# Turning raw exponentials in forgetting and latent attention, and dividing by their sums after the value product

## What is computed

```
sb = (jnp.einsum('bhqd,bhkd->bhqk', sl(qb), kb).astype(jnp.float32) * scale
      + (c_q[..., None] - cum[:, :, None, :]))
pb = jax.nn.softmax(jnp.where(causal, sb, -jnp.inf), axis=-1)
ob = jnp.einsum('bhqk,bhkd->bhqd', pb.astype(vb.dtype), vb)
```

```
s = (jnp.einsum("bqhd,bkhd->bhqk", qn, k_nope)
     + jnp.einsum("bqhr,bkr->bhqk", qp, k_pe)).astype(jnp.float32) * MLA_SCALE
s = jnp.where(kpos[None, :] <= qpos[:, None], s, NEG)
p = jax.nn.softmax(s, axis=-1).astype(v.dtype)
return jnp.einsum("bhqk,bkhd->bqhd", p, v)
```

## Time and profile before

| | |
|---|---|
| median of 3 runs | 2430.66 us |
| span of the profiled execution | 2425.54 us |
| TensorE busy | 2388.7 us (98%) |
| VectorE, ScalarE, GpSimd busy | 51%, 39%, 41% |
| chain that ended last | TensorE 91%, VectorE 3%, ScalarE 2% |
| fox, first score to last value product | 194.67 to 362.81 us: 168.14 us |
| mla0, the same | 1708.04 to 1762.10 us: 54.06 us |
| mla1, the same | 1788.81 to 1843.37 us: 54.56 us |

### The profile page before, as it was taken

One profiled execution on the slowest core, in us unless ns is written; L12 is line 12 of the kernel. 1 busy time (PEld: TensorE's weight loads), 2 busy tenths in 40 slices (PEclk: granted clock), 3 DMA queues, 4 the chain that ended last, 5 costly groups with the idle time before them and its releaser, 6 DMA issues.

```text
span 2425.5 us, 29219 instructions
## 1 busy us (share of the span) xinstructions
PE 2388.7 (98%) x10762; PEld 1877.3 (77%) x10762; DVE 1237.2 (51%) x2086; ACT 952.3 (39%) x1438; POOL 1000.8 (41%) x744
## 2 busy tenths in 40 slices
PE   8999999999999999999999999999989999999999
PEld 6777668877888888857878888887556877888887
DVE  4453545334334436794456455556765334555454
ACT  3354345433322226524444222226766434222223
POOL 4323224333454445635425554544021233554443
PEclk9999999999999999999999999999999999999999
DMA  5212213421322233222223223232102421322331
GB/s 171 87 53 83 83 43 122 157 87 53 126 91 100 88 103 104 87 70 88 86 59 103 100 92 104 87 104 68 36 18 87 147 97 53 107 93 88 102 104 70
DMA packets 169703, 218.31 MB, mean 90 GB/s; under 512 B 6584, under 2 KB 143338, under 8 KB 169590
## 3 DMA queue, kind: packets, MB, share of 16 engines
q1 hardware_dynamic: 168278, 214.59, 27.2%
q10 hardware_dynamic: 1312, 2.21, 0.3%
HBM read 214.66 MB, written 2.12 MB: 89 GB/s over the span
## 4 chain that ended last, share of the span: by engine, by line
PE 91%; DVE 3%; ACT 2%; issue 1%; POOL 1%; DMA 1%; SPq 0%; DVEq 0%; ACTq 0%
PE ps_l L839 78%; PE ps_l L1096 3%; PE ps_l L988 2%; PE ps_s L1146 2%; PE ps_l L1222 1%; POOL w_lo L685 1%; PE ps_s L1205 1%; ACT w_hi L1444 1%; PE ps_s L1309 1%; PE ps_s L1324 1%; PE ps_s L1111 1%; DVE small L2752 0%; PE ps_s L839 0%; DVE arena L2235 0%; DVE a_lo L2287 0%
## 5 line engine op out<-in xcount | busy, mean ns | idle before, releaser
L685 POOL TENSOR_TENSOR w_lo<-w_raw,w_hi 128x512 fp32r<-128x512 f32 (+1 forms) x740 | 1000.6, 1384 | 1403.5 <-ACT w_hi L1444 1385.7
L839 PE MATMUL ps_l<-a_hi,w_hi 128*128 128x512 f32 x1936 | 763.6, 394 | 2.9 <-POOL w_lo L685 2.8
L839 PE MATMUL ps_l<-a_lo,w_hi 128*128 128x512 f32 x1952 | 758.4, 389 | 0.0
L839 PE MATMUL ps_l<-a_hi,w_lo 128*128 128x512 f32 x1936 | 754.1, 390 | 0.0
L1444 ACT ACTIVATE w_hi<-w_raw 128x2048 fp32r<-128x2048 f32 (+2 forms) x196 | 370.6, 1891 | 587.7 <-PE ps_l L839 579.5
L839 PEld LDWEIGHTS ps_l<-a_hi,w_hi 128*128 128x128 f32 x1936 | 363.0, 188 | 88.0 <-issue 10.8
L839 PEld LDWEIGHTS ps_l<-a_lo,w_hi 128*128 128x128 f32 x1952 | 366.0, 187 | 78.0 <-issue 3.1
L839 PEld LDWEIGHTS ps_l<-a_hi,w_lo 128*128 128x128 f32 x1936 | 362.7, 187 | 77.3
L839 PE MATMUL ps_l<-b_hi,w_hi 128*128 128x512 f32 (+1 forms) x892 | 329.4, 369 | 6.2 <-POOL w_lo L685 3.8
L839 PE MATMUL ps_l<-b_hi,w_lo 128*128 128x512 f32 (+1 forms) x892 | 326.7, 366 | 0.0
L839 PE MATMUL ps_l<-b_lo,w_hi 128*128 128x512 f32 (+1 forms) x892 | 326.7, 366 | 0.0
(11 more groups left out here) (294 smaller groups left out, 2509.1 us busy)
## 6 DMA issues: line engine op xcount, KB each, us to landing
w_raw<-in_ffn_w_up_dram SPq DMA_DIRECT2D x44, 1024.0 KB, 5.0
w_raw<-in_w_dram SPq DMA_DIRECT2D x32, 1024.0 KB, 5.2
w_raw<-in_ffn_w_down_dram SPq DMA_DIRECT2D x22, 1024.0 KB, 4.9
w_raw<-in_w_in_dram SPq DMA_DIRECT2D x20, 1024.0 KB, 5.3
w_raw<-in_xa_wkv_dram SPq DMA_DIRECT2D x16, 1024.0 KB, 5.5
w_raw<-in_w_kv_mem_dram SPq DMA_DIRECT2D x8, 1024.0 KB, 5.6
w_raw<-in_xa_wq_dram SPq DMA_DIRECT2D x8, 1024.0 KB, 5.1
w_raw<-in_xa_wo_dram SPq DMA_DIRECT2D x8, 1024.0 KB, 5.2
```

The lines of the kernel that those rows point to most:

```text
L685: e.tensor_tensor(w_lo[:, b % 2, o], w_raw[:, b % 2, o], w_hi[:, b % 2, o].bitcast(F32), ALU.subtract).then_inc(w_lo_made[by], 1)
L839: ins = pe.matmul(o, *((v, w) if swap else (w, v)), start=first and n == 0, stop=last and n == 2)
```

## The change

Both attentions turn the raw exponentials, not the divided ones, and the division by the sums comes after the value product. For that the value product is made the other way round: the turned block is the stationary operand and the values (64 columns) move, 10 products per head, so that the result has queries on its rows. VectorE multiplies it with the reciprocals of the sums while it takes it out of PSUM (P), TensorE turns the result back (a new event W, four tiles for two heads), and O and the low part (Q) work on two heads at once, 128 x 512.

In fox two heads become one event: 16 steps, not 32; S scores both heads of a pair one after the other on the upper and the lower 64 rows of the array; T turns both; the lag is 2 steps; the fills are dealt out anew over the 19 steps. The rows of sums come for two heads in one DMA, with a small one ahead for block 0.

In mla heads stay single; the lag is 2 steps instead of 3, V follows T of the last block by one event step and stands behind T of the next head's block 0; P two steps after T, W and O (for odd heads) two, Q three. The buffers for exponentials and for turned blocks are doubled, so exponentials no longer wait for the turning of the head before.

```diff
+def latent_events(heads, lag):
+    for step in range(n + lag + 4):
+        for kind in "PQ":
+            if (step, kind) in due:
+                ev.append((kind, due[step, kind], 0))
+        if step < n:
+            ev.append(("S", *divmod(step, TT)))
+        for kind in "WO":
+            if (step, kind) in due:
+                ev.append((kind, due[step, kind], 0))
+        if lag <= step < n + lag:
+            h, i = divmod(step - lag, TT)
+            ev.append(("T", h, i))
+            if i == TT - 1:
+                due[step + 1, "V"] = due[step + 2, "P"] = h
+                if h % 2:
+                    due[step + 2, "W"] = due[step + 2, "O"] = due[step + 3, "Q"] = h // 2
+        if (step, "V") in due:
+            ev.append(("V", due[step, "V"], 0))
...
-    attention("fox", FOX_HEADS, 3, "v", 1, extra="K", after=(2, 2, 3), fills=(
+    attention("fox", FOX_HEADS, 2, "v", 2, extra="K", after=(1, 2, 2, 3, 3), pairs=True, fills=(
...
+            def pair_values(g, p, _):
+                claim(pe, L, g)
+                wait_read(pe, L, plan.events["fox"][1]["T", p, TT - 1] + 1)
+                for i, e in itertools.product(range(TT), (0, 1)):
+                    o = P * i + 64 * e
+                    for k in range(i + 1):
+                        ins = pe.matmul(bank(L, g)[:, o:o + 64], pt_pair(i)[:, e, k, :],
+                                        vb[:, k, (2 * p + e) * 64:(2 * p + e + 1) * 64], start=k == 0, stop=k == i)
+                ins.then_inc(l_full, 1)
+            def pair_values_turned(g, p):
+                claim(pe, L, g)
+                wait_read(pe, L, plan.events["fox"][1]["V", p, 0])
+                for i in range(TT):
+                    ins = turn(bank(L, g)[:, i * P:(i + 1) * P], o_fox(p)[:, i, :])
+                ins.then_inc(l_full, 1)
...
+            def masked_scores(g, i, both):
+                n = P * (i + 1)
+                for e, (q, k) in enumerate(both):
+                    claim(pe, S, g + e)
+                    pe.matmul(bank(S, g + e)[:, 0:n], q, k[:, 0:n] if n < T else k, start=True, stop=False)
+                for e in (0, 1):
+                    pe.matmul(bank(S, g + e)[:, i * P:n], ident_bf[:, :], mask_bf[:, :], start=False, stop=True)\
+                        .then_inc(s_full, 1)
...
+                    if kind == "V":
+                        claim(pe, L, g)
+                        wait_read(pe, L, at["T", h, TT - 1])
+                        for q in range(TT):
+                            for k in range(q + 1):
+                                ins = pe.matmul(bank(L, g)[:, 64 * q:64 * q + 64], pt_lat(h, q, k),
+                                                vh[:, k, h * 64:(h + 1) * 64], start=k == 0, stop=k == q)
+                        ins.then_inc(l_full, 1)
...
+                    if kind == "P":
+                        wait_read(dve, S, at["S", h, TT - 1])
+                        rl4, l = lat_sum[:, 4 * TT:5 * TT], TT * (h % 4)
+                        step(dve.reciprocal(rl4, lat_sum[:, l:l + TT]))
+                        wait_group(dve, L, g)
+                        if h >= 4:
+                            wait_group(dve, L, at["W", h // 2 - 2, 0])
+                        sync()
+                        dve.tensor_tensor(o_lat(h // 2)[:, :, 64 * (h % 2):64 * (h % 2) + 64],
+                                          bank(L, g)[:, 0:4 * 64].rearrange("p (q d) -> p q d", d=64),
+                                          rl4.unsqueeze(2).broadcast_to((P, TT, 64)), ALU.mult).then_inc(l_free["v"], 1)
```

More of the change, by code:

```diff
@@ L122, in attention_events, with pair_events, turned_groups @@
     return ev
+def pair_events(pairs, lag, extra, after, fill):
+    ev = []
+    n = pairs * TT
+    due = {}
+    for step in range(n + lag + 8):
+        if step < n:
+            p, i = divmod(step, TT)
+            if "K" in extra and step == 0:
+                ev.append(("K", 0, 0))
+            ev.append(("S", p, i))
+            if "K" in extra and p and i == 0:
+                ev.append(("K", p, 0))
+            if "K" in extra and i == 1 and p + 1 < pairs:
+                ev.append(("K", p + 1, 1))
+        for kind in "POQ":
+            if (step, kind) in due:
+                ev.append((kind, due[step, kind], 0))
+        for item in fill.get(step, ()):
+            ev.append(("G", item, 0))
+        for kind in "WV":
+            if (step, kind) in due:
+                ev.append((kind, due[step, kind], 0))
+        if lag <= step < n + lag:
+            p, i = divmod(step - lag, TT)
+            ev.append(("T", p, i))
+            if i == TT - 1:
+                for kind, wait in zip("VPWOQ", after):
+                    due[step + wait, kind] = p
+    return ev
+def turned_groups(i):
+    return 1 if i < 2 else 2
+def latent_events(heads, lag):
+    ev = []
+    n = heads * TT
+    due = {}
+    for step in range(n + lag + 4):
+        for kind in "PQ":
+            if (step, kind) in due:
+                ev.append((kind, due[step, kind], 0))
+        if step < n:
+            ev.append(("S", *divmod(step, TT)))
+        for kind in "WO":
+            if (step, kind) in due:
+                ev.append((kind, due[step, kind], 0))
+        if lag <= step < n + lag:
+            h, i = divmod(step - lag, TT)
+            ev.append(("T", h, i))
+            if i == TT - 1:
+                due[step + 1, "V"] = due[step + 2, "P"] = h
[3 more added lines that the diff above has]
+            ev.append(("V", due[step, "V"], 0))
+    return ev
 class Plan:
@@ L195, in attention @@
     def attention(name, heads, lag, score_who, per_score, t_who="a", v_who="v", v_groups=1, extra="",
-                  after=(3, 3, 4, 3, 3), fills=(), halves=()):
+                  after=(3, 3, 4, 3, 3), fills=(), halves=(), pairs=False):
         fill = {}
@@ L201, in attention @@
                 fill.setdefault(step, []).append((tag, *divmod(n, parts), parts))
-        ev = attention_events(heads, lag, extra, after, fill, halves)
+        ev = pair_events(heads // 2, lag, extra, after, fill) if pairs else \
+            attention_events(heads, lag, extra, after, fill, halves)
         at = {}
@@ L214, in attention @@
                 at[kind, h, i] = len(L.who)
-                L.who += [t_who]
+                L.who += [t_who] * (turned_groups(i) if pairs else 1)
             elif kind == "V":
@@ L223, in attention @@
                     L.who += [next(who for t, *_, who, _, _ in fills if t == tag)]
-            elif kind in "OPN":
-                at[kind, h, i] = at["V", h, i]
+            elif kind in "OPNQ":
+                at[kind, h, i] = at["W" if pairs and kind in "OQ" else "V", h, i]
         p.events[name] = (ev, at)
@@ L328, in make_plan @@
         p.weights(f"uk{half}", "mla_w_ukv_2", 2, 1024, [(0, 1024 * half)], 8)
-        attention(f"mla{half}", 8, 3, "a", 1)
+        ev, at = latent_events(8, 2), {}
+        for kind, h, i in ev:
+            ring, who = {"S": (S, "a"), "T": (L, "a"), "V": (L, "v"), "W": (L, "v")}.get(kind, (None, ""))
+            if ring:
+                at[kind, h, i] = len(ring.who)
+                ring.who.append(who)
+            else:
+                at[kind, h, i] = at["V" if kind == "P" else "W", h, 0]
+        p.events[f"mla{half}"] = (ev, at)
     feat_around("mla_o", "mla_w_o_2", [0, 256, 512, 768], "memT2")
@@ L1062, in _, with attention @@
             ins.then_inc(s_full, 1)
-            def attention(name, score, values, before=None, turned=None, subln=None, fills={}):
+            def attention(name, score, values, turned=None, subln=None, values_turned=None, fills={}):
                 ev, at = plan.events[name]
@@ L2281, in half_values, with walk_pairs @@
[L2281 to L2288, removed]
+            def walk_pairs(scores, evict, low, filled):
+                ev, at = plan.events["fox"]
+                for kind, p, i in ev:
+                    g = at[kind, p, i]
+                    if kind == "S":
+                        scores(g, p, i)
+                    if kind == "G" and ring_who(g) == "v" and p[2] == p[3] - 1:
+                        filled(g, *p[0:2])
+                    if kind == "P":
+                        evict(g, p)
+                    if kind == "Q":
+                        low(g, p)
```

235 lines of the change are left out of this document (170 added, 65 removed).

## The result

The changed kernel takes 2493.07 us (median of four runs, 2489.25 to 2493.46) against 2430.55 us: +62.5 us, a ratio of 1.0252 (95% interval 1.0238 to 1.0267). The forecast had the sign, +15.6 us, and a range up to 2456. The profiled execution has a span of 2491.6 us.

A forecast was written before the change was run, and what follows sets the result against it. Fox was taken as bound by TensorE's work, mla by a loop through three in-order engines. Fox -11.8 and mla +27.4 gave +15.6 us on 2430.7: 2446 us, range 2434 to 2456.

The forecast's parts named there:

- the 27.4 of the sum: Both latent attention (mla) halves together: predicted 27.4 us slower, 68.0 us per half against 54.1 and 54.6; bounds +20 to +33.
- Nothing else can move except by being pushed: Whole kernel: the change touches only fox and the two mla halves, so other stretches were given no cost.
- Fox: Forgetting attention: scores -11.8, losses around them -2.7, turning back +1.8, open end +0.9, together -11.8 us; bounds -15 to -7.
- rival 2: Fox: the two scores of a pair don't overlap, fox gains about 0, kernel at 2458 us; chance 5%.
- What I took as hidden: Fox: the score-to-turning chain, DMAs for pairs' rows and ScalarE's queue lie under other work, costing nothing.
- Values: Both attentions' value products: 20 records per head, each bound by its 0.115 us weight load, 2.3 us, no change.
- The loop: mla: from V's end to the next V's end nothing overlaps, 7.64 us per head, 9.24 every second head.
- Rival 1: mla: the loop doesn't close, mla stays bound by TensorE, and the kernel takes 2417 us; chance 12%.
- rival 3: mla: TensorE's clock falls; at 1.2 GHz a half's 48 us of work double, kernel beyond 2490 us; chance 2%.

## Why the prediction was wrong, and what of it held

The whole difference, taken apart by differences of medians:

| | us |
|---|---|
| fox (2418.01 less 2430.5) | -12.5 |
| latent attention's order, clock full (2450.91 less 2418.01) | +32.9 |
| the clock (2466.53 less 2450.91) | +15.6 |
| the place of a2 (2493.07 less 2466.53) | +26.5 |
| sum | +62.5 |

The second line holds the added products too, and the third is what they buy net of their own cost; only the sum of the two, 48.5 us, is free of them. The line of the place is good to some 3 us: the same kind of difference is 23.2 us for 96 bytes in the kernel before and 20.8 us for 128 bytes with fox alone (2438.78 less 2418.01).

The forecast was 46.9 us short. The place, which stood in no term, is 26.5 of them, the clock 15.6; latent attention's order took 5.5 more than the 27.4 of the sum (added products included), and fox gave 0.7 more.

**What bounds the kernel: one sentence failed.** "Nothing else can move except by being pushed" is the step where most was lost. I read what the change executes and not what it allocates: the line `lat_sum = sb(...)` stands in the diff and was costed at nothing. Some 3,500 products read a2 (88 groups of 24 products in the up parts of the two gated feed-forwards, 32 groups in the MLP, 24 in the queries of the three cross-attentions: 144 x 24), and 6 to 7 ns more for each is 21 to 24 us. No row of the trace of before could have given the price; the warning was that every high, low and weight tile stood at the same place modulo 256 bytes, and that the new tile's 96 bytes are no multiple of that.

**Fox: held.** -11.8 us worked out, -11.8 measured against the runs beside it (2418.01 less 2429.80). The agreement to a tenth is luck: the interval of that ratio allows 9 to 17 us, and the stretch itself became 13.8 us shorter, 154.3 us where I had 156. A pair's score of 128 columns takes 0.43 us to the masks, where one head alone had been put at 0.42, and TensorE's wait ahead of the last W is 0.88 us where I had 0.9 (the changed kernel's rows of the start and the end of fox):

```profile
196.56 0.49 PE L1300 MATMUL ps_s<-arena 64*128 64x128 f32 x4
196.99 0.28 PE L1302 MATMUL ps_s<-mask_bf,ident_bf 128*128 128x128 bf16 x2
...
350.18 0.69 DVE L2512 TENSOR_TENSOR arena<-ps_l,lat_sum 128x512 f32<-128x512 f32 x1 [3.54 <-PE ps_l L1236]
351.02 0.63 PE L1103 MATMUL ps_l<-keep,arena 128*128 128x128 f32 x4 [0.88 <-DVE arena L2512]
```

The overlap of two row halves carried over from differential attention, so rival 2 is out. What I took as hidden (DMAs of pairs, banks, ScalarE's queue) was hidden: TensorE was busy 153.58 of the stretch's 154.34 us.

**Values: held.** 20 records in 2.26 us, against 2.3 from the one-column rows; making the values the moving operand bought nothing.

**The loop: held, to a tenth.** 7.53 us against 7.64, 9.14 against 9.24, with O and Q ahead of the next maximum as worked. The first V starts 7.3 us after the first score (1712.14 to 1719.41), 7.4 expected. With the clock full the halves took 71.9 us with the added products; 68.0 was the sum, and no run has this order at full clock without these products. The two runs with another order (2411.5 and 2422.9 us) show that it is the list and neither the new form of the values nor W that costs. Rival 1 had the loop not closing and 2417 us; it was wrong of this order, but once the order is loosened the form gives even 2411.5.

**The clock: rival 3, dismissed with 2%, is the other step that failed.** It came true in part: 0.81 on the mean of a half, not 0.5 throughout. My evidence against it was that the clock had stayed full "with their waits". But those halves were busy 92% of their time, and the ones forecast only 5.9 of 8.4 us, 70%; no row of before showed such a stretch of mla at any clock, and the range should have carried that. Nor was the clock always full before: the earlier trace rows is one execution. The run with the spare 256 bytes is as fast as the kernel before and executes the same instructions, and in its profiled execution mla0 (first score to last V) had

```profile
1710.47:1765.78 55.31, 51.43 (x241) 28.71 (x241) 41.08 (x135) 37.65 (x104) 3.04 (x4) 0.97 0.06 20
```

The mean of 0.97 is a short fall of the clock behind TensorE's waits of 1.65, 0.80 and 0.47 us at the start of this half. So the kernel before already showed, on a small scale, what rival 3 describes.

The Trainium skill (TensorE: Matmul & The Clock Gate, section "🎯 Why this matters for your kernels") names an idle gap between bursts of matmuls as what throws the clock back, and the gap that it gives is longer than any wait in these halves: in those of the changed kernel the clock fell with no single wait above 1.2 us just ahead of it, only several in a row. The Trainium skill's sentence (same page, "Part 4: PE-mode transpose") that transposes don't count as activity like other products would fit, since turned tiles are much of what lies between these waits, but no run here separates them; the run with V and T later turned the same tiles with the clock at 1.00 and TensorE busy 48.63 of 50.29 us.

The sum was also built in a way that hid this: its terms were priced at full clock, and then the clock was given a chance of its own as if the two were independent. They weren't. It was the loop's waits that left TensorE idle, and with the waits filled (2450.91 us) or removed (2411.50 us) the clock stayed up.

## What to carry to other kernels

Read the allocations of a diff as well as its instructions: an unused tile of 96 bytes cost 23 us in a kernel of 2430. When a change moves a consumer closer to its producer in an order written by hand, write out the loop from that consumer's end to its next start over all in-order queues; if it closes, loosen the order before judging the new form. And when the sum itself says that TensorE will be idle for nearly a third of a stretch, price the stretch at a lower clock too.

## What the runs showed of the hardware

- Products of 512 columns (high and low parts of float32) started 226 to 227 ns apart when moving and stationary tiles started alike modulo 256 bytes, and on average 232 to 237 ns apart when the moving tiles had been shifted by 96 bytes against the weights, 233 by 128 bytes; moving all tiles together cost nothing (2430.47 us). Whether the weights are the partner that matters was not separated, and other offsets weren't tried.
- TensorE's clock fell to its lower level (1.2 GHz) after a stretch in which it had been busy 6.8 of 8.9 us and its longest wait was 1.1 us, and twelve small products per head placed ahead of such waits kept it at 2.4 GHz: 15.6 us gained by doing more.
- Two float32 score products on the upper and the lower 64 rows of the array cost together what one costs alone, 0.43 us at 128 columns against 0.41 for one in the kernel before, also where a mask product on all 128 rows follows.
